# Halved down products, 512-column first iterations and two-pass sums of squares in a tuned two-block transformer kernel

## The reference, cut to what matters

```python
def rmsnorm(x, g):
    xf = x * lax.rsqrt(jnp.mean(x * x, axis=-1, keepdims=True) + EPS)
    return xf * g

def swiglu(h, w_gate, w_up, w_down):
    return (jax.nn.silu(h @ w_gate) * (h @ w_up)) @ w_down

# first block: two layers, model width 1024, 512 tokens and 16 meta tokens (528 in all)
h = h + 0.5 * swiglu(rmsnorm(h, ffn1_norm[l]), ...)   # FFN 0 (l = 0), FFN 2 (l = 1)
h = h + mixer(rmsnorm(h, mix_norm[l]))                # pooling (l = 0), latent attention (l = 1)
h = h + 0.5 * swiglu(rmsnorm(h, ffn2_norm[l]), ...)   # FFN 1 (l = 0), FFN 3 (l = 1)
# after layer 0: keys and values from rmsnorm(h, kv_in_norm); at the end rmsnorm(h, final_norm)
# second block: 512 tokens
u = rms_norm(x, mix_norm_g)                           # proj = u @ w_in, three branches, gates
x = x + merged @ w_o
x = x + (silu(gt) * up) @ w_ffn_out                   # FFN 4, hidden width 2816 like the others
```

## Time and profile before

| what | value |
|---|---|
| median of three runs | 2399.51 us (2398.27 to 2400.09) |
| the profiled execution's own time: its span from first to last instruction | 2396.0 us |
| TensorE busy | 2387.8 us, 16268 matmuls |
| VectorE busy | 1566.9 us |
| ScalarE busy | 1452.6 us |
| mean DMA rate | 168 GB/s |

### The profile page before, as it was taken

How to read it: one execution, slowest core, us unless ns; L and a number is a source line. 1 busy time by engine, 2 the same in 40 slices (tenths; PEclk the granted TensorE clock), 3 DMA queues, 4 the chain that set the end, 5 groups by cost and what they waited for, 6 DMA issues and landing times.

```text
span 2396.0 us, 40147 instructions
## 1 busy us (share of the span) xinstructions
PE 2387.8 (100%) x16268; PEld 2193.6 (92%) x16268; DVE 1566.9 (65%) x2190; ACT 1452.6 (61%) x1914; POOL 281.3 (12%) x330
## 2 busy tenths in 40 slices
PE   9999999999999999999999999999999999999999
PEld 9999999999999999998689999977778888999998
DVE  8756656867565867675778576654786533776664
ACT  7547466554476575477775564766875565654743
POOL 0101010110011010011001110111011111110101
DMA  7658594685588486688346776986556888575866
GB/s 217 162 141 204 146 225 95 150 221 124 141 203 212 124 207 162 159 208 208 77 89 173 197 168 160 233 186 145 123 125 162 189 186 192 130 180 156 206 159 155
DMA packets 244345, 401.37 MB, mean 168 GB/s; under 512 B 12304, under 2 KB 170896, under 8 KB 244160
## 3 DMA queue, kind: packets, MB, share of 16 engines
q0 software_dynamic: 46944, 170.94, 38.9%
q1 hardware_dynamic: 197216, 227.85, 29.7%
HBM read 225.73 MB, written 2.10 MB: 95 GB/s over the span
## 4 chain that ended last, share of the span: by engine, by line
PE 97%; DVE 1%; DMA 1%; ACT 1%; issue 0%; SPq 0%; DVEq 0%; ACTq 0%
PE ps L677 45%; PE ps L816 40%; PE ps L760 4%; PE ps L1150 1%; PE ps L1186 1%; PE ps L1174 1%; PE ps L1195 1%; PE ps L1062 1%; PE ps L1026 1%; PE ps L1046 1%; PE ps L886 1%; PE ps L865 0%; DMA raw<-in_ffn_w_up 0%; PE ps L917 0%; PE ps L709 0%
## 5 line engine op out<-in xcount | busy, mean ns | idle before, releaser
L816 PE MATMUL ps<-xbH,wH 128*128 128x256 f32 (+1 forms) x2806 | 784.2, 280 | 0.6 <-DMA wL<-raw 0.5
L816 PE MATMUL ps<-xbL,wH 128*128 128x256 f32 (+1 forms) x2800 | 782.3, 279 | 0.0
L816 PE MATMUL ps<-xbH,wL 128*128 128x256 f32 (+1 forms) x2800 | 782.3, 279 | 0.0
L816 PEld LDWEIGHTS ps<-xbH,wH 128*128 128x128 f32 x2806 | 526.5, 188 | 1.4 <-issue 0.6
L816 PEld LDWEIGHTS ps<-xbL,wH 128*128 128x128 f32 x2800 | 526.2, 188 | 0.4
L635 POOL DMA_DIRECT2D wL<-raw x326 | 281.1, 863 | 2086.6 <-ACT wL L1272 2067.9
L816 PEld LDWEIGHTS ps<-xbH,wL 128*128 128x128 f32 x2800 | 525.6, 188 | 0.0
L1272 ACT ACTIVATE wL<-raw 128x1024 fp32r<-128x1024 f32 x326 | 343.8, 1055 | 174.0 <-PE ps L677 131.5
L1290 ACT ACTIVATE wH<-raw 128x1024 fp32r<-128x1024 f32 x375 | 392.5, 1048 | 79.4 <-PE ps L677 50.9
L1286 ACT ACTIVATE wH<-wS 128x1024 fp32r<-128x1024 f32 x200 | 212.0, 1060 | 344.9 <-DVE wS L1825 327.2
L677 PE MATMUL ps<-aH,wL 128*128 128x256 f32 (+1 forms) x1226 | 348.9, 331 | 0.0
(11 more groups left out here) (316 smaller groups left out, 3228.0 us busy)
## 6 DMA issues: line engine op xcount, KB each, us to landing
wL<-raw POOLq DMA_DIRECT2D x326, 512.0 KB, 5.6
raw<-in_ffn_w_gate SPq DMA_DIRECT2D x88, 512.0 KB, 5.3
raw<-in_ffn_w_up SPq DMA_DIRECT2D x88, 512.0 KB, 6.0
raw<-in_ffn_w_down SPq DMA_DIRECT2D x88, 512.0 KB, 5.4
raw<-in_w_in SPq DMA_DIRECT2D x56, 512.0 KB, 4.3
raw<-in_w_ffn_in SPq DMA_DIRECT2D x44, 512.0 KB, 5.4
raw<-in_w_ffn_out SPq DMA_DIRECT2D x22, 512.0 KB, 5.4
raw<-in_w_o SPq DMA_DIRECT2D x12, 512.0 KB, 5.5
```

What stands on the lines that cost most here:

```text
L816: ins = nc.tensor.matmul(ps[:, 2 * s + j, 0:TH], lhs, rhs, start=begin, stop=p in (2, 3, 4) and k == KP - 1 and q == 2, skip_group_check=True)
```

## The change

Three things are changed. In FFN 2 to 4 each down product's matmul of 512 columns becomes two of 256 into the same bank with the same weights, but for the six matmuls of the first pair and the first output block of each part. Their first iterations use one matmul of 512 columns in place of two of 256 (96 matmuls in place of 192), and the repeated matmuls (`again`, line 851) are taken out. Ten sums over partitions (f1, dkv, kv, dq, f3, final, b2, mean, lnv, f4) are made of two f32r passes: ScalarE writes the high part of the total (`total_high`), VectorE the low rest (`total_low`), both into idle scratch, and TensorE multiplies each with ones that ScalarE makes once, at the start, out of the matrix of minus ones. The matrix of ones is no longer loaded.

```diff
+        onesR = place("onesR", [P, P], F32R)
...
-            def product(s, T, wcol, sl, rhs, start, stop):
+            def product(s, T, wcol, sl, rhs, start, stop, halved=False):
                 parts = [(0, CUT), (CUT, T1)] if T == T1 else [(0, T)]
+                if halved:
+                    parts = [(0, T // 2), (T // 2, T)]
...
-                        to = CUT if T == T1 and c == 0 else 0
-                        ins = nc.tensor.matmul(ps[:, 2 * s + c, to:to + b - a], lhs, r[:, a:b],
-                                               start=start and n == 0, stop=stop and n == 2,
+                        bank, to = (0, a) if halved else (c, CUT if T == T1 and c == 0 else 0)
+                        ins = nc.tensor.matmul(ps[:, 2 * s + bank, to:to + b - a], lhs, r[:, a:b],
+                                               start=start and n == 0 and not (halved and c), stop=stop and n == 2,
...
+            def split_stats(p, T, s):
+                pe.wait_ge(dve_done, at("dve", f"ssl:{p}"))
+                parts = totals[totals_in.get(p, "sq")]
+                cuts = [(0, CUT), (CUT, T1)] if T == T1 else [(0, SEQ)]
+                for e in range(2):
+                    for c, (a, b) in enumerate(cuts):
+                        bank, to = (c, CUT if c == 0 else 0) if T == T1 else (0, a)
+                        ins = nc.tensor.matmul(ps[:, 2 * s + bank, to:to + b - a], onesR[:, :], parts[:, e, a:b],
+                                               start=e == 0, stop=e == 1, skip_group_check=True)
+                done(ins, f"st:{p}")
...
+                            if f > 1:
+                                ins = nc.tensor.matmul(pairs(ps[:, 2 * s, 0:T]), lhs, x[:, b:b + 2, k, :],
+                                                       start=e == k == q == 0,
+                                                       stop=e == 1 and k == KP - 1 and q == 2,
+                                                       skip_group_check=True)
+                                continue
...
-                                        again = f > 1 and 0 < part < 3 and begin and p == 2 and it == n - 1 and j == 0
-                                        for _ in range(1 + again):
...
-                                    if f > 2 and part == 0 and dg == 1 and d == 1 and fl == 0:
-                                        nc.tensor.matmul(ps[:, 2 * sl[d], 0:T], wH[:, (u + n) % RING, d * P:d * P + P],
...
-                                                  (aH[:, fl, :], aL[:, fl, :]),
-                                                  fl == 0, fl == 2 * n - 1)
+                                                  (aH[:, fl, :], aL[:, fl, :]), fl == 0, fl == 2 * n - 1,
+                                                  f > 1 and (dg, d, fl // 2) != (0, 0, 0))
...
+            def total_high(p, T, ev):
+                on_dve(ev)
+                total = rl if p == "b2" else ss
+                fn(nc.scalar.activation(totals[totals_in.get(p, "sq")][:, 0, 0:T], total[:, 0:T], ACT.Copy), f"ssh:{p}")
...
+            act.wait_ge(s_c, 16)
+            fn(nc.scalar.activation(onesR[:, :], none_, ACT.Copy, scale=-1.0), "ones")
             high(4)
...
             for k in range(KP):
                 scaled_block(3, k, ("ffn2_norm1",))
+                if k == 1:
+                    total_high("f3", SEQ, f"ss:f3:{KD - 1}")
...
+            def total_low(p, T):
+                on_act(f"ssh:{p}")
+                total, parts = rl if p == "b2" else ss, totals[totals_in.get(p, "sq")]
+                do(V.tensor_tensor(parts[:, 1, 0:T], total[:, 0:T], f32(parts[:, 0, 0:T]), ALU.subtract), f"ssl:{p}")
...
             for k in range(KP):
                 difference(3, k)
+                if k == 2:
+                    total_low("f3", SEQ)
```

More of the change, by code:

```diff
@@ L61 @@
 POOL_W = (2, 4, 8, 16)
-C_ID, C_NTRI, C_NONE, C_ONE, C_HEAD, C_MASK = (i * P for i in range(6))
-C_MAIN = 6 * P
+C_ID, C_NTRI, C_NONE, C_HEAD, C_MASK = (i * P for i in range(5))
+C_MAIN = 5 * P
 BAND = 2 * P
@@ L327, in program @@
         sq = place("sq", [P, 2, T1])
+        totals = {"t1": place("t1R", [P, 2, T1], F32R, z1), "t2": place("t2R", [P, 2, T1], F32R, z1 + 2 * T1 * 4),
+                  "sq": place("sqR", [P, 2, T1], F32R, z1 + 6 * T1 * 4)}
+        totals_in = {"dq": "t1", "b2": "t2"}
         small = place("small", [P, 16 + 3 * NH])
@@ L473, in f32 @@
             return ap.bitcast(F32)
+        ones = f32(onesR[:, :])
         def gcol(name, k):
@@ L937, in _ @@
                     done(ins, f"dkv:u{j}")
-            norm_stats("dkv", T1, group("st:dkv"))
+            split_stats("dkv", T1, group("st:dkv"))
             ffn(2)
@@ L1129, in _ @@
                 if n == 0:
-                    for p, src, n_ahead in (("final", ss, 0), ("b2", rl, 1)):
-                        s = group(f"st:{p}", None, ahead(n_ahead))
-                        stats(f"st:{p}", s, [src[:, 0:SEQ]], ones, f"ss:{p}:{KD - 1}")
+                    for p, n_ahead in (("final", 0), ("b2", 1)):
+                        split_stats(p, SEQ, group(f"st:{p}", None, ahead(n_ahead)))
                 if n == 2:
@@ L1226, in _ @@
                     if turn == 1 and p == 0:
-                        stats("st:mean", group("st:mean"), [ss[:, 0:SEQ]], ones, "convs")
+                        split_stats("mean", SEQ, group("st:mean"))
                     if turn == 1 and p == 1:
-                        stats("st:lnv", group("st:lnv"), [ss[:, 0:SEQ]], ones, f"ss:ln:{CT - 1}")
+                        split_stats("lnv", SEQ, group("st:lnv"))
             count[0] = 0
@@ L1550, in _ @@
                 plain_block(2, k, ("ffn1_norm1",))
+                if k == 2:
+                    total_high("dkv", T1, f"ss:dkv:{KD - 1}")
                 if k < 2:
@@ L1639, in _ @@
                 scaled_block(3, k, ("ffn2_norm1",))
+                if k == 1:
+                    total_high("f3", SEQ, f"ss:f3:{KD - 1}")
             ffn(3, ("ffn2_norm1",), "final")
+            for p in ("final", "b2"):
+                total_high(p, SEQ, f"ss:{p}:{KD - 1}")
             for n in range(4):
@@ L1748, in _ @@
                     after("br", j, f"gate{b}:u{U0['br'] + j}")
+                    if turn == 1 and p < 2:
+                        total_high(("mean", "lnv")[p], SEQ, ("convs", f"ss:ln:{CT - 1}")[p])
                     after("br", j + 1, f"gate{b}:{2 * p + 1}")
@@ L1983, in first_gating, with both @@
                 r = norm(f).rearrange("p (c n) -> p c n", c=2)
+                def both(what):
+                    s = C.slot.get(f"{name}:{what}", 0)
+                    return halves(s, T) if f < 2 else pairs(ps[:, 2 * s, 0:T])
                 def gates():
@@ L1987, in gates @@
                         on_pe(f"{name}:g2.{j}")
-                        do(V.tensor_tensor(pairs(t1[:, j, 0:T]), halves(C.slot.get(f"{name}:g{j}", 0), T), r, ALU.mult),
+                        do(V.tensor_tensor(pairs(t1[:, j, 0:T]), both(f"g{j}"), r, ALU.mult),
                            f"rd:{name}:g{j}", f"{name}:g{j}")
@@ L1994, in ups @@
                         on_act(f"{name}:silu{j}")
-                        do(V.scalar_tensor_tensor(pairs(m[:, j, 0:T]), halves(C.slot.get(f"{name}:u{j}", 0), T), -1.0,
+                        do(V.scalar_tensor_tensor(pairs(m[:, j, 0:T]), both(f"u{j}"), -1.0,
                                                   pairs(t2[:, j, 0:T]), ALU.mult, ALU.mult),
@@ L2003, in first_gating @@
                     sum6(f, k, gain)
+                if f == 1:
+                    total_low("f1", T)
                 if f:
@@ L2226, in _ @@
                 plain_block(2, k, ("ffn1_norm1",))
+                if k == 2:
+                    total_low("dkv", T1)
                 if k < 3:
@@ L2362, in _ @@
                 difference(3, k)
+                if k == 2:
+                    total_low("f3", SEQ)
             ffn(3, ("ffn2_norm1",), "final")
+            for p in ("final", "b2"):
+                total_low(p, SEQ)
             on_pe(f"qk:u{U0['qk']}")
@@ L2583, in _ @@
                         scaled(t1[:, e, 0:SEQ], f"gate{b}:{2 * p + e}", SEQ)
+                    if turn == 1 and p < 2:
+                        total_low(("mean", "lnv")[p], SEQ)
                     if turn == 0:
```

30 lines of the change are left out of this document (19 added, 11 removed).

## The result

The changed kernel takes 2421.61 us (median of four runs, 2421.04 to 2422.04); the kernel before took 2398.89 us beside it (four runs, 2397.63 to 2400.09). The ratio is 1.0089 with a 95% interval of 1.0076 to 1.0103: slower by 22.7 us. The prediction (2385.7, range 2384 to 2410) missed, in sign and in range. It is the time that the rival with three slow FFNs gave (2421.7 us), which had a chance of 0.06. One execution of all those reported here, in the first experiment, was slow for another reason (granted clock 0.65, 3837.64 us) and is left out.

The account below looks back on a forecast made before the run. TensorE's matmul issue was taken as the bound. All at the fast pace, -4.0 - 1.6 - 1.1 - 3.3 - 2.2 - 2.25 + 0.2 + 0.5 = -13.8 us gave 2385.7 us, range 2384 to 2410.

Parts of the forecast that it names:

- the rival with three slow FFNs: Rival: three FFNs fall into the slow pace at 12.0 us each, giving 2421.7 us; chance 0.06.
- The reading of the pace: 256-column matmuls take 113.3 or 117.8 ns, set by a period-three step of the last 512-column matmul ahead; a hypothesis.
- The sums: Ten sums in two f32r passes: -4.0 us, with the added ScalarE and VectorE work costed at nothing on the path.
- First iterations: First iterations of FFN 2 to 4 in 96 matmuls of 512 columns, 21.97 us each: -1.6 us.
- Repeats gone: Six repeated matmuls of 256 columns and two of 512 (line 851) taken out: -1.1 us.
- Halving: 1494 down matmuls halved in FFN 2 to 4: -3.3 us at the fast pace (taken), +10.0 at the slow one.
- The pace of everything else: Later iterations of part 0 and FFN 4's part 1 turn fast, -2.2 and -2.25 us; other bound +6.7 us.
- The constant at the start: ScalarE's copy making the ones at the kernel's start: between nothing and +0.3 us, taken as +0.2.
- Part 0: With TensorE earlier, waits for weights in part 0 can grow: 0 to 2 us, taken as 0.5.
- the first rival: One FFN falls into the slow pace and stays there, costing 12.0 us: 2397.7 us; chance 0.24.
- pairs never fast: Rival: halved down pairs stay slow because weights are loaded twice, the rest goes fast: 2399 us; chance 0.07.
- VectorE's chain in part 0: Rival: VectorE's chain takes over in part 0, 0.7 us per sum in FFN 1, 3, 4: 2388 us; no separate chance.

Follow-up runs that it names:

- the first experiment: The changed kernel keeping 5, 4 and 4 down matmuls of 512 columns instead of 6 in part 0 of FFN 2, 3 and 4: 2396.68 us.
- the versions with and without the repeated half: The changed kernel with three groups of six whole down matmuls in part 0 of FFN 2 to 4; one half repeated between groups: 2391.37 us; none: 2421.81 us.
- the halving alone: The kernel before with halved down products, six kept whole per part, and the repeat at line 851 taken out; f32 sums and first iterations as before: 2396.04 us.
- the sums alone: The kernel before with the ten sums in two f32r passes and nothing else changed: 2408.21 us.
- the first iterations alone: The kernel before with 96 matmuls of 512 columns in the first iterations of FFN 2 to 4, nothing else changed: 2400.62 us.
- the repeats alone: The kernel before without its eight repeated matmuls (six of 256 columns, two of 512), nothing else changed: 2406.42 us.

## Why the prediction was wrong

The reading of the pace was right, and it is now shown: paces of 113.3 and 117.8 ns, set, where the cycle runs, by the step of the last 512-column matmul, handed on by counts that are multiples of three, some 10 us for each slow FFN (30 us between the versions with and without the repeated half). What failed is the step from that reading to a chance. By the parts of the prediction:

1. *The sums:* the size was right (0.46 and 0.49 us each, -4.0 in all), and the engines' extra work is hidden, nearly as costed. (It was put at 26 us; ten copies and ten subtractions are 10 x (0.616 + 0.693) = 13.1 us, and the pages show 7.3 and 7.0 us more on ScalarE and VectorE.) But costing the sums by their own length alone was wrong: alone they make the kernel 10 us slower. The heads say where. In FFN 2 there was no wait ahead of part 0's down products, and their run ended on 394; with the two-pass sum a wait of 0.2 us stands there, and it ends on 388. In FFN 3 the run came out one step further on, and the repeated matmul of line 851, which had moved 392 to 394, now moved 394 to 388. FFN 4 fell in the middle of part 1.
2. *First iterations:* -1.1 instead of -1.6 us. The term that was off is FFN 2's, 22.40 for 21.97: it took 229 ns a matmul from the second block, though here the two-pass sum of 256 and 272 columns stands ahead of it.
3. *Repeats gone:* a term of -1.1 us that was really +8 (one run). The prediction saw that they had lifted FFN 4 (505 against 504) and still booked them as mere work.
4. *Halving:* both bounds were right: -3.3 us at the fast pace (with the halving alone a down piece takes 32.65 us against 32.96), +10.0 at the slow one (9.9 measured). The slow end came.
5. *The pace of everything else:* the other bound, all of parts 1 to 3 slow, came in all three FFNs (+17.4 us in the balance, since FFN 4's part 1 was slow before), and the 4.45 us of gain did not come. This and item 4 are nearly the whole miss.
6. *The constant at the start:* nothing shows.
7. *Part 0:* the waits were there, 0.3 to 0.5 us at the head of the down products, within the 0 to 2 us. What was not costed is that such a wait sets the step anew. Of the 18 heads of six matmuls in the traces with the two-pass sums, ten ended on 392, eight on 388, none on 394. In the halving alone, with f32 sums, FFN 3's ended on 392, but FFN 2's, with no wait ahead, and FFN 4's ended on 394.

The sentence that failed is in the first rival: FFN 3's "36 + 2 + 60 more end on 394, fast, if nothing stalls at 1271". The count failed ahead of any stall: it takes the two matmuls of a two-pass sum as two steps. In the changed kernel the 36 ended on 389 and the 60 behind the sum on 389 again (388 within a ns), so a two-pass sum entered on 388 moves nothing, and FFN 3's part 0 was slow at once. Then came the stall, which the earlier trace rows already showed at 1271, since 54 x 228.9 ns is 12.36 us and not 12.62. FFN 4's "it ends on 388, slow" came true, but by luck. By its count the 72 matmuls behind the first sum end on 394; they ended on 388 (at 1928.6, by form), and so did each stretch behind it:

```profile
L684 PE MATMUL ps<-hcH,wL 128*128 128x512 f32 x1 | 0.4, 388 | 0.0
```

Three sums counted as two each make six, a multiple of three, so the error fell out. With that the three FFNs are not independent draws with a good chance each: behind the new sums all three reach part 0's down products on a slow step, the waits at the heads of this kernel and its versions never gave 394, and nothing behind them could lift an FFN. The condition was written down for one FFN and should have made "three slow" the likeliest case. That a run behind a wait can come out on 394, FFN 3 of the sums alone shows (54 matmuls behind a wait of 0.3 us); what decides it stays open.

Of the rivals, *pairs never fast* fell with the halving alone. With it falls what was left of the rule of the Trainium skill (TensorE: Matmul & The Clock Gate, "Back-to-back issue gap"), one fixed gap on top of the columns for any length, which that section itself gives for a matmul by itself and not for a stream. This stream doesn't follow it: 256 columns take 113.3 or 117.8 ns and 512 columns 228.9 or 233.3, by what stands ahead. *VectorE's chain in part 0* does show (2% of the chain against 1%; in FFN 3 the chain runs over VectorE and ScalarE from 1253.88 to 1279.45), but costs no more than the half microsecond of the head's wait.

## What to carry to other kernels

Before you take out a matmul that seems to do nothing, or change a count in a long run, find out from the chain whether it holds the rest of the run at its better pace; price it by all that stands behind it. Where a pace hangs on a state that is handed on, ask of each wait what state it leaves, and put something that mends it (here one repeated half in each gap between kept groups, in every FFN) behind the last wait rather than ahead of it. And a kernel that runs at the better pace is the less steady one: one matmul 30 to 90 ns late can cost it several us, while the changed kernel, slow throughout, repeats within 1 us.

## What the runs showed of the hardware that was not expected

- TensorE keeps a step over hundreds of matmuls. In a stretch at 117.8 ns each matmul of 256 or 512 columns moves it on by one of three; one more matmul in part 0 decides the pace of 1836 behind it (8.2 us).
- 512 columns have two steady paces too: 228.9 ns (388, 392, 394 recorded in turn) and 233.3 ns (397 or 398 throughout), the second seen over 96 matmuls behind a two-pass sum of 256 and 272 columns, and in the changed kernel over 24 behind the 512-column one at 1123.9.
- The two matmuls of a two-pass sum that is entered on 388 leave the step where it is: the 72, 624 and 60 matmuls behind such sums all ended on 388 or 389.
- A single matmul 30 to 90 ns late turned a fast 256-column run into a slow one from there on, in all three cases traced (58.69 us for 504 in one). A longer stop needn't: of sixteen, of 0.1 to 1 us, ten left the run fast (0.5 us at 2140.9 in the halving alone) and six made it slow (FFN 3's part 1 in the first iterations alone). A late one in a stretch at 117.8 ns moved the step as well, for the better in one case (the repeats alone) and for the worse in another.
- Why there are three steps, why the one recorded with 394 ns is followed by the fast pace, and which wait leaves which step, no run here shows.
